# First layer's experts: three buffers for gate and up, two for down, each filled by one transfer

## The chip, the cores and the metric

The kernel runs on one core of one Trainium2 chip. The metric is the device time of one execution in microseconds (us), as the median of several runs. All matrices are in 32-bit floating point.

## The reference, cut to what matters

The model is two transformer blocks behind each other. The change lies in the mixture-of-experts part of the second block, which has two layers. Each layer routes its tokens to two of 32 experts (512 tokens in the first layer, 256 in the second), and each expert is three weight matrices of 2 MB each:

```python
def expert_block(args):
    xe, e = args
    return (jax.nn.silu(xe @ w_gate[e]) * (xe @ w_up[e])) @ w_down[e]
...
y = lax.map(expert_block, (xb, blk_e)).reshape(cap, d)
out = jax.ops.segment_sum(y.astype(jnp.float32) * w_buf[:, None], tok_buf, num_segments=t + 1)
```

`w_gate[e]` and `w_up[e]` are 1024 x 512, `w_down[e]` is 512 x 1024. With at most 64 rows for each expert the kernel makes 32 expert steps in a layer, and reads 96 matrices, 201 MB.

## The kernel before, in words

All work is written out by hand for each engine, with semaphores between them. One expert step `e` on TensorE (`pair`, L1472) is: the first half of the gate and up products (`hidden`), the transposes of the last expert's activation (`turn_act`), the second half of the gate and up products, the transposes of the next expert's rows (`turn_rows`, first layer only), and then the down products of expert `e - 1` (`down`, L1457). So the down weights of an expert are used one step later than its gate and up weights. `hidden` signals `pe_hidden`, and `down` signals `pe_y_hi`.

The weights are loaded by SyncE (SP) on one queue, in the order of its program. A buffer for one matrix is called a home. Each of the three parts (0 gate, 1 up, 2 down) has homes 0 and 1 in the six ring slots (`MOE_SLOTS`), and in the first steps of a layer also more homes in memory that is idle then: gate's home 2 is `hT`, up's home 2 is in the arena, down's home 2 is made of three rows of `more` and one of `hb`, and gate's home 3 is made of pieces, in the first layer the three rows of `bc`, `silu_fix` and a part of the arena (`gate_pieces`). A home made of pieces is filled by one transfer for each piece (`fetch_pieces`, L674): down's home 2 by four of 512 KB, gate's home 3 by three of 512 KB and two of 256 KB. All other homes are filled by one transfer of 2 MB (`fetch`, L667).

`HOMES = (4, 3, 3)` says how many homes gate, up and down have. The class `Homes` plays the first steps through (16 in the first layer, 28 in the second: `UNROLLED`) and writes the list `refills`: which matrix goes to which home, and which signal SP waits for before it (L736 to L738). After those steps each part goes by homes 0 and 1 alone, in a loop (`pair` of SP, L693): it waits for `pe_hidden` of `e` and loads gate and up of `e + 1`, then waits for `pe_y_hi` of `e - 1` and loads down of `e`. So that the loop finds its homes, the last matrices of the list must lie in the home of their number's parity (the condition `f < any_home or h == f % 2` in `freed`).

Before the first step, SP's `experts` (L661) fills all homes: homes 0 and 1 as the output projection `w_o` frees the ring, gate's home 2 and the pieces when `homes_dead` tells that the attention's memory is free (L722 to L726), and up's home 2 and the last piece of gate's home 3 after the first gathered rows have landed (L731 to L734). The rows of each expert in the first layer are gathered by GpSimd (POOL) from DRAM, and every expert's output is stored by it with an indirect DMA. The second layer gathers nothing.

Of the kernel before, what the change touches and what calls it, by code (L numbers as in the profile page):

```python
# [21 lines left out]
NB = 512  # L22
# [99 lines left out]
def build_program(nc, I, out):  # L122
    with ExitStack() as ctx:
        def sb(name, shape, dt=F32):
            return ctx.enter_context(nc.sbuf_tensor("sb_" + name, shape, dt))
# [26 lines left out]
        xs = sb("xs", [P, 4, D])  # L152
        bc = sb("bc", [P, 3, D])
# [7 lines left out]
        silu_fix = sb("silu_fix", [P, NB])  # L161
# [31 lines left out]

        MOE_SLOTS = ((2, 3, 4), (0, 1, 5))
        UNROLLED = (16, 28)
        HOMES = (4, 3, 3)

        def loop_sems(l):
            by_rows = ["places", "equals", "marked"] if l else ["rows0", "rows1", "picked_in"]
# [76 lines left out]
        for p, what in enumerate(loads):  # L276
            if 0 <= p - loads_to[0] < LAND:
                q = behind_experts[p - loads_to[0]]
            else:
                q = min(range(LAND), key=lambda q: -1 if held[q] is None else turn[held[q]])  # L280
# [15 lines left out]
        def steps_less_2(engine):  # L296

            return engine.value_load(steps_i[0:1, 0:1], min_val=N_EXP // 2 - 2, max_val=CAP // ROWS * (N_EXP // 2) - 2)

        def expert_steps(engine, v, body, l, first=True, between=None):  # L300

            if first:
                for i in range(UNROLLED[l] // 2):
                    body(i, False)
            if between:
                between()
            with engine.Fori(UNROLLED[l] // 2, v + 1) as i:
                body(i, False)
            body(v + 1, True)
# [9 lines left out]
        class Homes:  # L319

            def __init__(self, n):
                self.n = n
                self.at, self.count, self.held, self.refills = {}, {}, {}, []
                self.next = list(HOMES)
                for part in range(3):
                    for e in range(HOMES[part]):
                        self.put(part, e, 1 - e if e < 2 else e)
                for e in range(n):  # L330
                    self.freed((1, 0), "pe_hidden", e)
                    if e:
                        self.freed((2,), "pe_y_hi", e - 1)
                self.first_held = {(part, j): self.held[part, j] for part in range(3) for j in range(2)}
# [24 lines left out]

                return max(0, self.last_at(part, j) - self.first_held[part, j])  # L360

        homes = [Homes(n) for n in UNROLLED]

        def moe_home(h, part):

            return ring[MOE_SLOTS[h][part]][:] if h < 2 else (hTf, view(8192, SLOT))[part]

        def gate_pieces(l):

            if l:  # L370
                return xs[:, 2, :], xs[:, 3, :], bc[:, 1, :], bc[:, 0, :]
            return bc[:, 0, :], bc[:, 1, :], bc[:, 2, :], silu_fix[:], view(5632, NB)

        def down_rows(h):

            if h == 2:
                return more[:, 0, :], more[:, 1, :], more[:, 2, :], hb[:, 0, :]
            return [moe_home(h, 2)[:, k * D:(k + 1) * D] for k in range(4)]

        def rows_by_k(l, part, h):  # L380

            pieces = gate_pieces(l) if h == 3 else [moe_home(h, part)]
            return [v[:, at:at + NB] for v in pieces for at in range(0, v.shape[-1], NB)]

        def transfers(l, part, h):

            return len(gate_pieces(l)) if h == 3 else 4 if (part, h) == (2, 2) else 1

        def slot_of(n):

# [12 lines left out]
        def view(at, *dims):  # L403
            n = int(np.prod(dims))
            v = A[:, at:at + n]
            if len(dims) == 1:
                return v
            names = "abcde"[:len(dims)]
            return v.rearrange(f"p ({' '.join(names)}) -> p {' '.join(names)}", **dict(zip(names, dims)))
# [133 lines left out]
        def rows_of(t):  # L543

            return own_y[:, t, :, :] if t < 2 else y_rows[:, t, :, :]
# [71 lines left out]
        def _(sp):  # L617
# [43 lines left out]
            def experts(l):  # L661


                m = moe[l]
                w3 = I["w_gate_2"][l], I["w_up_2"][l], I["w_down_2"][l]

                def fetch(part, h, e):  # L667

                    src = w3[part][e:e + 1, :, :] if isinstance(e, int) else w3[part][bass.ds(e, 1), :, :]
                    src = src.rearrange("o (p k) n -> p (o k) n", p=P)  # L670
                    dst = moe_home(h, part).rearrange("p (k n) -> p k n", k=src.shape[1])
                    sp.dma_start(dst, src).then_inc(m[f"landed{3 * h + part}"], 16)  # L672

                def fetch_pieces(part, h, e, which):  # L674

                    src = w3[part][e].rearrange("(p k) n -> p (k n)", p=P)
                    at = 0
                    for q, dst in enumerate(gate_pieces(l) if h == 3 else down_rows(h)):
                        n = dst.shape[-1]
                        if q in which:  # L680
                            sp.dma_start(dst, src[:, at:at + n]).then_inc(m[f"landed{3 * h + part}"], 16)
                        at += n

                def refill(part, h, e):

                    if transfers(l, part, h) > 1:
                        fetch_pieces(part, h, e, range(transfers(l, part, h)))
                    else:
                        fetch(part, h, e)

                of = lambda n: n if isinstance(n, int) else n % N_EXP

                def pair(i, last):  # L693
                    for j in range(2):
                        e = i * 2 + j
                        if not (last and j == 1):

                            sp.wait_ge(m["pe_hidden"], e)
                            fetch(0, 1 - j, of(e + 1))
                            fetch(1, 1 - j, of(e + 1))  # L700

                        sp.wait_ge(m["pe_y_hi"], e - 1)
                        fetch(2, j, of(e))


                if l == 1:
                    sp.wait_ge(s["homes_dead"], 2)
                    fetch_pieces(0, 3, 3, range(4))
                fetch_pieces(2, 2, 2, range(3))

                n0 = first[f"w_o{l}"]
                idle = idle_at[l]
                behind = [slot_at[place["w", n0]], LAND + n0 % 2]
                waiting = [(0, 1), (1, 1), (0, 0), (1, 0), (2, 1), (2, 0)]
                for used, slots in ((turn["w", n0] + 1, idle), (turn["w", n0 + 1] + 1, behind), (uses_to[l], None)):
                    sp.wait_ge(s["w_used"], used)
                    now = [(part, h) for part, h in waiting if slots is None or MOE_SLOTS[h][part] in slots]
                    for part, h in now:
                        fetch(part, h, 1 - h)
                        waiting.remove((part, h))  # L720

                sp.wait_ge(s["homes_dead"], 1 + 2 * l)  # L722
                fetch(0, 2, 2)
                fetch_pieces(2, 2, 2, (3,))
                if l == 0:
                    fetch_pieces(0, 3, 3, range(4))  # L726
                sp.wait_ge(s["steps_ready"], l + 1)
                less_2 = steps_less_2(sp)
                steps = less_2 + 2
                if l == 0:  # L730
                    sp.wait_ge(m["rows0"], 16)  # L731
                fetch(1, 2, 2)
                if l == 0:
                    fetch_pieces(0, 3, 3, (4,))  # L734

                for part, e, h, signal, count in homes[l].refills:  # L736
                    sp.wait_ge(m[signal], count)
                    refill(part, h, e)  # L738
                expert_steps(sp, less_2, pair, l, first=False)

                def rows(t):

                    sp.dma_start(rows_of(t), DR["y"][l][2 * t * P:2 * (t + 1) * P, :].rearrange("(p j) d -> p j d", j=2)).then_inc(s[f"y_loaded{t}"], 16)

                sp.wait_ge(s["y_stored"], 1 + 2 * l)
                rows(0)
                if l == 0:
                    sp.wait_ge(m["pe_hidden"], steps * 2 - 1)
                    load(loads_to[0])
                rows(1)  # L750
                if l == 0:
                    load(loads_to[0] + 1)
                    sp.wait_ge(s["y_stored"], 2)
                    sp.wait_ge(s["own_w"], OWN_READY)
                    rows(2)
                    rows(3)
# [2607 lines left out]
```

## Time and profile before

| | us |
|---|---|
| median of 3 runs | 2381.54 (2381.46 to 2382.77) |
| the profiled execution | 2383.17 |
| its span on the core | 2381.4 |
| TensorE busy | 2163.0 (91%) |
| VectorE busy | 1108.3 (47%) |
| first layer's experts | about 1204 to 1700 |
| second layer's experts | about 1895 to 2375 |

The span is what the records of the engines cover; the execution's own time is 1.8 us more. A time in a row counts from the start of the span. "DMA share" is the mean busy share of the 16 DMA engines, and "q1" is SP's queue, "q0" that of GpSimd. The granted clock is given as a share of 2.4 GHz.

### The profile page before, as it was taken

How to read it: one execution, taken by the hardware profiler on the slowest of the kernel's cores; microseconds unless marked ns; L12 is line 12 of the kernel's file. 1: busy time of each engine (PE TensorE's matmuls, PEld its weight loads, DVE VectorE, ACT ScalarE, POOL GpSimd, SP SyncE). 2: the span in 40 equal slices, each digit the busy share in tenths (PEclk: the TensorE clock that was granted, in tenths of full speed). 3: DMA queues.
4: the chain of work that ended last, by engine and by line, in shares of the span. 5: the costliest groups of instructions: out<-in, count | busy, mean ns of one | idle time of the engine just before them, and what ended most of it. 6: DMA issues, size and time to landing. Idle time of an engine off the chain costs nothing. (4 is left out here: it accounts for less than half of the span.)

```text
span 2381.4 us, 28791 instructions
## 1 busy us (share of the span) xinstructions
PE 2163.0 (91%) x11404; PEld 1359.2 (57%) x11404; DVE 1108.3 (47%) x1760; ACT 692.2 (29%) x1102; POOL 215.2 (9%) x318
## 2 busy tenths in 40 slices
PE   8899999998899999988979887888788899999987
PEld 6778788876777888865733332333365533333332
DVE  5677654465677546477521111111488522222223
ACT  4243344344334433257111101011237211111110
POOL 2000000010000001100011111111120100000000
PEclk9989999999999999999889998999889899999999
DMA  9745576573655656611699999999861699999996
GB/s 308 257 150 188 193 237 203 173 282 126 242 204 187 216 181 215 181 51 35 254 345 393 405 411 392 406 409 407 317 151 63 239 399 425 426 425 425 426 416 274
DMA packets 186570, 657.08 MB, mean 276 GB/s; under 512 B 17511, under 2 KB 63159, under 8 KB 164304
## 3 DMA queue, kind: packets, MB, share of 16 engines
q1 hardware_dynamic: 170592, 622.66, 68.6%
q0 software_dynamic: 14032, 30.00, 4.0%
q10 hardware_dynamic: 1824, 2.73, 0.3%
q8 instruction: 86, 1.41, 0.2%
q14 instruction: 36, 0.29, 0.0%
HBM read 649.97 MB, written 23.79 MB: 283 GB/s over the span
## 5 line engine op out<-in xcount | busy, mean ns | idle before, releaser
L811 PE MATMUL bank<-sb_ring_rounded,sb_hT_rounded 128*128 128x512 f32 x2432 | 605.0, 397 | 17.0 <-DVE sb_ring_rounded L2112 6.6
L811 PEld LDWEIGHTS bank<-sb_ring_rounded,sb_hT_rounded 128*128 128x128 f32 x2432 | 458.4, 191 | 117.9 <-issue 11.8
L1443 PE MATMUL bank<-sb_ring,sb_arena 128*64 128x512 f32 x1472 | 431.3, 633 | 63.3 <-DMA sb_ring<-in_w_up 51.1
L2112 DVE TENSOR_TENSOR sb_ring_rounded<-sb_ring,sb_ring_rounded 128x2048 fp32r<-128x2048 f32 (+1 forms) x142 | 314.9, 2258 | 111.3 <-ACT sb_ring_rounded L1584 106.3
L811 PE MATMUL bank<-sb_ring_rounded,sb_arena_rounded 128*128 128x512 f32 x1408 | 356.7, 395 | 7.7 <-DVE sb_arena_rounded L2099 7.2
L1584 ACT ACTIVATE sb_ring_rounded<-sb_ring 128x2048 fp32r<-128x2048 f32 x146 | 268.0, 1887 | 123.9 <-PE bank L811 98.9
L811 PEld LDWEIGHTS bank<-sb_ring_rounded,sb_arena_rounded 128*128 128x128 f32 x1408 | 266.0, 190 | 63.5 <-DVE sb_arena_rounded L2099 7.4
L1443 PEld LDWEIGHTS bank<-sb_ring,sb_arena 128*64 128x64 f32 x1472 | 130.0, 144 | 253.3 <-issue 241.2
L1994 ACT ACTIVATE sb_hb<-bank 64x512 f32<-64x512 f32 x64 | 37.8, 591 | 659.1 <-PE bank L1443 659.1
L1467 PE MATMUL bank<-sb_ring,sb_arena 128*64 128x512 f32 x800 | 191.5, 622 | 18.6 <-issue 15.0
L2946 DVE COPY sb_arena<-bank 128x256 f32<-128x256 f32 x64 | 27.2, 424 | 279.0 <-PE bank L1454 268.9
L2969 DVE COPY sb_arena<-bank 64x512 f32<-64x512 f32 x64 | 44.4, 693 | 201.1 <-PE bank L1443 201.1
L1467 PEld LDWEIGHTS bank<-sb_ring,sb_arena 128*64 128x64 f32 x800 | 57.6, 142 | 121.6 <-issue 117.8
L1443 PE MATMUL bank<-sb_arena 128*64 128x512 f32 x232 | 104.7, 596 | 0.0
L3146 POOL DMA_INDIRECT scratch_y<-sb_arena,sb_pick x62 | 57.1, 922 | 407.4 <-DVE sb_arena L2953 178.7
L2955 DVE TENSOR_TENSOR sb_arena<-bank,sb_bc 64x512 f32<-64x512 f32 x32 | 22.2, 693 | 141.4 <-PE bank L1467 141.4
L1443 PE MATMUL bank<-sb_hT,sb_arena 128*64 128x512 f32 x176 | 79.8, 596 | 6.5 <-DMA sb_arena<-in_w_up 3.3
L2953 DVE COPY sb_arena<-bank 64x512 f32<-64x512 f32 x30 | 20.8, 693 | 122.4 <-PE bank L1467 122.4
L3216 POOL TENSOR_TENSOR sb_st<-sb_st,sb_cst 128x1 f32<-128x1 f32 x32 | 25.2, 789 | 522.8 <-DVE sb_st L2094 389.6
L1689 ACT ACTIVATE sb_hb<-bank,sb_st 128x512 f32<-128x512 f32 (+1 forms) x96 | 61.3, 652 | 19.1 <-DVE sb_st L2319 13.2
L1454 PEld LDWEIGHTS bank<-sb_cst,sb_arena 64*128 64x128 f32 x256 | 35.4, 210 | 52.7 <-issue 52.7
L1563 ACT ACTIVATE sb_hT_rounded<-bank 128x512 fp32r<-128x512 f32 x56 | 31.7, 599 | 107.4 <-PE bank L847 104.7
(376 smaller groups left out, 2379.4 us busy)
## 6 DMA issues: line engine op xcount, KB each, us to landing
sb_ring<-in_w_up SPq DMA_DIRECT2D x50, 2048.0 KB, 22.0
sb_ring<-in_w_down SPq DMA_DIRECT2D x50, 2048.0 KB, 24.1
sb_ring<-in_w_gate SPq DMA_DIRECT2D x42, 2048.0 KB, 21.9
sb_ring<-in_w_ada SPq DMA_DIRECT2D x48, 1024.0 KB, 7.3
sb_ring<-in_ffn_w_gu SPq DMA_DIRECT2D x44, 1024.0 KB, 7.8
sb_arena<-in_w_up SPq DMA_DIRECT2D x14, 2048.0 KB, 24.3
sb_hT<-in_w_gate SPq DMA_DIRECT2D x11, 2048.0 KB, 29.0
sb_more<-in_w_down SPq DMA_DIRECT2D x42, 512.0 KB, 23.9
```

Source lines behind the costliest of these rows:

```text
L811: ins = pe.matmul(bank[b][0:rows, :], rnd(x), rnd(w[:, k, :]), start=start and k == k0 and q == 0, stop=stop and k == k1 - 1 and q == len( ...
L1443: ins = pe.matmul(bank[2 * j + part][part * ROWS:(part + 1) * ROWS, :], mxT[:, j, k, :], w[part][k], start=k == 0, stop=k == KD - 1)
L1454: ins = pe.transpose(bank[2 * j][:, k * ROWS:(k + 1) * ROWS], mact[0:ROWS, j, k:EXP_H:4], ident[0:ROWS, 0:ROWS])
L1467: ins = pe.matmul(bank[S0 + n][n * ROWS:(n + 1) * ROWS, :], mactT[:, j, k, :], w[k][:, n * NB:(n + 1) * NB], start=k == 0, stop=k == 3)
L1563: act.activation(rnd(dst), bank[b][:, 0:n * P].rearrange("p (k n) -> p k n", k=n), ACT.Copy).then_inc(*c.up(s["x_hi"]))
L1584: act.activation(rnd(high_of(n)[:, k0:k1, :]), slot_of(n)[:, k0:k1, :], ACT.Copy).then_inc(*c.up(s["w_hi"]))
L1689: act.activation(j_e[:, g % 2, a, at:at + nk], bank[score_banks(g) + a][:, at:at + nk], ACT.Exp, bias=nm[:, h:h + 1], scale=query_rstd(t, ...
L1994: act.activation(msil[0:ROWS, j, :], bank[2 * j][0:ROWS, :], ACT.Silu).then_inc(m["silu"], 1)
L2112: dve.tensor_tensor(rnd(w), w, whole(high_of(n)[:, k0:k1, :]), ALU.subtract).then_inc(*c.up(s["w_lo"]))
L2946: dve.tensor_copy(mactT[:, j, :, :], bank[2 * j][:, 0:4 * ROWS].rearrange("p (k n) -> p k n", k=4)).then_inc(m["aT"], 1)
L2969: dve.tensor_copy(mup[0:ROWS, j, :], bank[2 * j + 1][ROWS:P, :]).then_inc(m["up"], 1)
L3146: pool.indirect_dma_start(out=DR["y"][l], out_offset=bass.IndirectOffsetOnAxis(ap=pick[:, 1, j:j + 1], axis=0), in_=my[0:ROWS, j, :], in_o ...
```

## The change

The first layer gets three homes for gate, three for up and two for down, in place of four, three and three. The homes made of pieces are no longer used in that layer. The second layer keeps its 4, 3 and 3 with their pieces.

```diff
-        HOMES = (4, 3, 3)
+        HOMES = ((3, 3, 2), (4, 3, 3))
...
-            def __init__(self, n):
+            def __init__(self, n, counts):
...
-                self.next = list(HOMES)
+                self.next = list(counts)
                 for part in range(3):
-                    for e in range(HOMES[part]):
+                    for e in range(counts[part]):
...
-        homes = [Homes(n) for n in UNROLLED]
+        homes = [Homes(n, counts) for n, counts in zip(UNROLLED, HOMES)]
...
-        def gate_pieces(l):
-            if l:
-                return xs[:, 2, :], xs[:, 3, :], bc[:, 1, :], bc[:, 0, :]
-            return bc[:, 0, :], bc[:, 1, :], bc[:, 2, :], silu_fix[:], view(5632, NB)
+        def gate_pieces():
+            return xs[:, 2, :], xs[:, 3, :], bc[:, 1, :], bc[:, 0, :]
...
                 if l == 1:
                     sp.wait_ge(s["homes_dead"], 2)
                     fetch_pieces(0, 3, 3, range(4))
-                fetch_pieces(2, 2, 2, range(3))
+                    fetch_pieces(2, 2, 2, range(3))
...
                 sp.wait_ge(s["homes_dead"], 1 + 2 * l)
                 fetch(0, 2, 2)
-                fetch_pieces(2, 2, 2, (3,))
-                if l == 0:
-                    fetch_pieces(0, 3, 3, range(4))
+                if l == 1:
+                    fetch_pieces(2, 2, 2, (3,))
...
                 fetch(1, 2, 2)
-                if l == 0:
-                    fetch_pieces(0, 3, 3, (4,))
```

The list of refills of the first layer becomes: up and gate of `e + 3` when the hidden products of `e` are done, down of `e + 2` when the down products of `e` are done. Its end is, with the signal and its count:

```
up, gate 15 pe_hidden 13    down 13 pe_y_hi 12
up, gate 16 pe_hidden 14    down 14 pe_y_hi 13    down 15 pe_y_hi 15 (home 1)
```

In the list before, the end is:

```
up, gate 14, pe_hidden 12 (gate 15, too)   down 14 pe_y_hi 12
up 15 pe_hidden 13    up, gate 16 pe_hidden 14    down 15 pe_y_hi 13
```

## Rows read from the trace of the kernel before

**Rows 1.** The windows view: busy time of each engine, then clock, DMA share, GB/s.
```profile
1220.00:1440.00 220.00, 193.30 (x898) 76.12 (x896) 37.41 (x60) 26.69 (x45) 31.81 (x46) 0.95 1.01 403
1480.00:1680.00 200.00, 169.03 (x748) 64.18 (x744) 30.35 (x49) 21.33 (x36) 26.86 (x49) 0.92 1.00 407
1960.00:2200.00 240.00, 237.89 (x1048) 88.09 (x1046) 65.75 (x114) 29.46 (x51) 19.83 (x35) 1.00 1.01 425
```

**Rows 2.** The waits view, TensorE, 1200 to 1700 us: total, times, longest, us.
```profile
PE bank L1443 <- DMA sb_ring<-in_w_up: 45.2, 16, 6.8
```

**Rows 3.** The timeline of TensorE, the first steps: start, duration, engine, line, operation.
```profile
1204.26 1.11 PE L1426 MATMUL bank<-sb_cst,sb_arena 64*128 64x64 f32 x8 [9.68 <-DMA sb_arena<-scratch_tokens,sb_spare]
1206.07 9.58 PE L1443 MATMUL bank<-sb_ring,sb_arena 128*64 128x512 f32 x32 [0.69 <-ACT sb_arena L1961]
...
1226.17 3.65 PE L1467 MATMUL bank<-sb_ring,sb_arena 128*64 128x512 f32 x16
...
1238.41 3.65 PE L1467 MATMUL bank<-sb_ring,sb_arena 128*64 128x512 f32 x16
```

**Rows 4.** The timeline of TensorE, the loop and the stage's end.
```profile
1492.66 3.65 PE L1443 MATMUL bank<-sb_ring,sb_arena 128*64 128x512 f32 x16 [1.80 <-DMA sb_ring<-in_w_up]
...
1508.89 6.62 PE L1443 MATMUL bank<-sb_ring,sb_arena 128*64 128x512 f32 x16 [3.76 <-DMA sb_ring<-in_w_up]
...
1692.44 3.60 PE L1467 MATMUL bank<-sb_ring,sb_arena 128*64 128x512 f32 x16
```

**Rows 5.** The timeline of SP's queue, the last fills and the first refills.
```profile
1182.58 0.33 SPq L672 DMA_DIRECT2D sb_hT<-in_w_gate  x1
1182.95 0.44 SPq L681 DMA_DIRECT2D sb_hb<-in_w_down  x1
1183.44 1.54 SPq L681 DMA_DIRECT2D sb_bc<-in_w_gate  x3
1185.02 0.46 SPq L681 DMA_DIRECT2D sb_silu_fix<-in_w_gate  x1
1204.04 0.34 SPq L672 DMA_DIRECT2D sb_arena<-in_w_up  x1
...
1215.69 0.33 SPq L672 DMA_DIRECT2D sb_ring<-in_w_up  x1
```

**Rows 6.** The DMA view, 1480 to 1680 us: packets, MB, share of 16 engines.
```profile
q1 hardware_dynamic: 5399, 78.58, 96.0%
```

**Rows 7.** The timeline of SP's queue, the list's end and the loop's first loads.
```profile
1406.62 5.18 SPq L672 DMA_DIRECT2D sb_ring<-in_w_down  x1
1431.35 0.36 SPq L672 DMA_DIRECT2D sb_ring<-in_w_gate  x1
...
1435.96 0.34 SPq L672 DMA_DIRECT2D sb_ring<-in_w_down  x1
```

**Rows 8.** The timeline of GpSimd, 1410 to 1460 us.
```profile
1438.38 1.72 POOL L3210 DMA_DIRECT2D sb_bc<-scratch_mod  x3
```

**Rows 9.** The timeline of SP's queue, the first fill of a home.
```profile
1143.77 0.33 SPq L672 DMA_DIRECT2D sb_ring<-in_w_gate  x1
```

**Rows 10.** The DMA view, 1142 to 1146 us, in slices of 0.1 us.
```profile
GB/s 0 0 0 0 0 0 0 0 0 0 0 0 0 0 0 0 0 0 0 0 0 0 0 0 0 0 0 1147 328 0 0 492 0 0 655 0 0 164 164 0
```

**Rows 11.** The timeline of GpSimd: the first gather.
```profile
1196.52 1.08 POOL L3134 DMA_INDIRECT sb_arena<-scratch_tokens,sb_spare  x1 [25.54 <-issue]
```

**Rows 12.** The tile view of the tokens in DRAM.
```profile
DMA to landing us min/median/max: 2.6/9.9/27.5
```

**Rows 13.** The windows view around the first gather.
```profile
1192.00:1200.00 8.00, 1.52 (x8) 0.90 (x8) 4.83 (x19) 0.00 (x0) 2.05 (x2) 0.63 0.99 403
1200.00:1208.00 8.00, 3.05 (x14) 1.66 (x16) 0.00 (x0) 1.88 (x2) 0.93 (x1) 0.50 0.82 152
```

**Rows 14.** The DMA view, 1220 to 1440 us.
```profile
q1 hardware_dynamic: 9234, 84.15, 95.3%
```

**Rows 15.** The timeline of SP's queue: the longest issue of pieces.
```profile
1299.11 24.50 SPq L681 DMA_DIRECT2D sb_bc<-in_w_gate  x3
```

More of the change, by code:

```diff
@@ L380, in rows_by_k @@
         def rows_by_k(l, part, h):
-            pieces = gate_pieces(l) if h == 3 else [moe_home(h, part)]
+            pieces = gate_pieces() if h == 3 else [moe_home(h, part)]
             return [v[:, at:at + NB] for v in pieces for at in range(0, v.shape[-1], NB)]
         def transfers(l, part, h):
-            return len(gate_pieces(l)) if h == 3 else 4 if (part, h) == (2, 2) else 1
+            return len(gate_pieces()) if h == 3 else 4 if (part, h) == (2, 2) else 1
         def slot_of(n):
@@ L677, in fetch_pieces @@
                     at = 0
-                    for q, dst in enumerate(gate_pieces(l) if h == 3 else down_rows(h)):
+                    for q, dst in enumerate(gate_pieces() if h == 3 else down_rows(h)):
                         n = dst.shape[-1]
```

## The prediction

> **What bounds the kernel now.** I read the page for the stages, then the windows view of the first layer's experts, then TensorE's waits there, and last the timelines of SP, TensorE and GpSimd at the two ends of the stage and where the list of refills hands over to the loop. From 1220 to 1680 us the DMA engines are full: share 1.01 and 1.00, 403 and 407 GB/s, while TensorE is busy 88% and 85% of the time at a granted clock of 0.95 and 0.92 [rows 1]. TensorE waits 45.2 us in this stage for up weights, in 16 waits [rows 2]. When nothing is late, one step takes TensorE 12.24 us (down products start at 1226.17 and at 1238.41 [rows 3]), so 32 steps would be done 392 us after 1206, near 1598; the last down products start at 1692.44 [rows 4]. So the stage is set by the bytes of SP's queue from the moment the queue is kept full, and a microsecond of idle DMA after that moment is a microsecond of the kernel. That moment is 1215.69, when the first step's gate and up products free their homes and the refills start [rows 5]. Before it the engines have slack: share 0.82 from 1200 to 1208 [rows 13].
>
> **The change, part by part.** The sum is made against the profiled execution: 2383.17 us, of which 2381.4 is the span. The median of the runs shown, 2381.54, is 1.6 us less than that execution.
>
> *Two homes less to fill ahead.* Gate 3 and down 2, 4.19 MB, were loaded before 1215.69, in time that the queue did not need. Now they are refills, behind it, and all other matrices queue as before. In the loop the queue moved 78.58 MB in 200 us [rows 6], or 0.393 MB for each us, so 2.10 MB take 5.34 us and the two 10.7 us. They lie in the path at full price, since the queue is full to the end. Bounds: 10.0 (at the 0.42 MB/us that the second layer's 425 GB/s would give [rows 1]) and 11.0 (at 84.15 MB in 220 us [rows 14]). In the first steps TensorE's pace holds: up and gate 3 are issued at 1215.69 and take 10.7 us, the third step's products need them at about 1242.
>
> *The handover.* Down has two homes, and the list must leave down 16 in home 0. So down 14 and down 15 both go to home 1, and SP waits with down 15 until the down products of expert 14 are done. Everything behind it in SP's program waits too: gate and up 17, down 16, though gate and up 17 have a free home before that. Down 14 is the last transfer in the queue then: gate and up 16 were issued a signal earlier. So the queue runs empty when down 14 has landed, and stays so for the start of the down products (some 0.3 us), their 3.65 us [rows 4], and the time from SP's issue to the first bytes, 0.9 us in the one case where the queue was empty: issued at 1143.77 [rows 9], first bytes in the slice at 1144.7 [rows 10]. With about 1 us from the last byte to the signal, an estimate, this is 6 us. Bounds: 4 (products and two short latencies at their least, and expert 14's store moving some bytes in the gap) and 9 (the clock has fallen in the wait: 16 products take 6.62 us then and not 3.65 [rows 4]). The 1.5 MB that GpSimd fetches into `bc` at this point do not fill the gap: they wait for the same down products, through expert 14's store (1438.38, right behind SP's issue at 1435.96 [rows 7, 8]). Before, nothing of this was there: down 15 was issued with expert 12's down products done, at 1406.62, and SP's pause until 1431.35 [rows 7] lay under a full queue [rows 1]. I take 6.0.
>
> *Fewer bytes in front of the first gather.* At 1182.58 SP issued gate 2 and then 2.36 MB of pieces [rows 5]. The first gather was issued at 1196.52 [rows 11], while the engines still were at 0.99 with SP's bytes [rows 13], and TensorE waited for it until 1204.26 [rows 3]. Without the pieces the queue is empty 5.6 us sooner (2.36 MB at 0.42), at about the gather's issue. The gather took 7.7 us; the shortest transfer on the same tensor took 2.6 us [rows 12]. Bounds: 0 and 5.1. I take 3, and all steps and refills start that much sooner, so it counts in full.
>
> *Whole transfers for pieces.* Gate's home 3 was refilled three times (experts 7, 11, 15) by five pieces, down's home 2 four times (5, 8, 11, 14) by four: 31 transfers become 7. While pieces were in flight the queue moved 84.15 MB in 95.3% of 220 us, 0.401 MB for each busy us; with none, 78.58 MB in 96.0% of 200 us, 0.409 [rows 14, 6]. The difference is 2% of 210 us, 4.3 us at most, and part of it comes with the denser gathers of the fast first steps. The other bound is nothing. I take 1.5 us, nearer to none: in the second layer, whose 240 us from 1960 are full of such pieces, the engines move 425 GB/s, more than here without any [rows 1]. SP's instructions for pieces that go away cost nothing: the queue is full while SP stands in them, as in the 24.50 us for three pieces [rows 15].
>
> *The rest.* The first three pieces of down 2, issued long before, left a stage with slack. VectorE, ScalarE and GpSimd do what they did. The second layer is unchanged and starts later by the sum.
>
> Sum: 10.7 + 6.0 - 3.0 - 1.5 = 12.2 us. 2383.2 + 12.2 = 2395.4 for a profiled execution, 2381.5 + 12.2 = 2393.7 for the median; I forecast 2394.
>
> **The rivals.**
>
> *Pieces are dear (faster).* Each transfer would cost the queue a time of its own that isn't under its neighbours, and 24 go. The price from a row is the 0.9 us from issue to first bytes: 24 x 0.9 = 21.6 us, so that the sum is 10.7 + 6.0 - 3.0 - 21.6 = -7.9 and the time 2373.6. It decides from 13.7 / 24 = 0.57 us for each piece. For it speaks that SP stood 24.50 us in three pieces [rows 15]. Against it speak the rates above: 31 pieces at 0.9 us would be 28 us of idle engines in 220, and the share is 1.01.
> The Trainium skill, "DMA: Bandwidth & Descriptors", section "Anatomy of one DMA", gives each DMA a fixed 2.0 us beside its bytes, and its section "Bandwidth" asks for transfers of 1 MiB and more. Taken for the queue and not for one transfer's latency, it would make 48 us of the 24, and the time about 2347; the trace has no room for this.
>
> *The gap is covered.* SP's queue does not run empty at the handover, because stores, gathers and the transfers of GpSimd fill it, or down 14 lands late enough. Then the sum is 10.7 - 3.0 - 1.5 = 6.2, the time 2388. Against it: down 15 cannot be issued before down 14 is used, whatever the speed.
>
> *TensorE becomes the bound in the first 16 steps.* With two homes, down weights land just ahead of their use, so a step waits twice. At the low clock 16 products take 6.6 us instead of 3.65 [rows 4], three such groups a step, and a step at the low clock throughout would be 12.24 + 3 x 2.97 = 21 us, above the 16 us of its bytes. If the clock fell for a third of each of the 12 steps that wait, they would have no slack left; for half of it, the excess is (12.24 + 4.5 - 16.0) = 0.7 us a step, 9 in all: 2403. Against it: a step has 3.8 us of idle in either kernel, and the clock was 0.92 with it.
>
> *Nothing changes.* The 4.19 MB would be loaded in slack again. This needs idle engines between 1216 and 1690, and there are none; only a start 12 us earlier could pay it, and the bound above is 5.1.
>
> **How the numbers follow.** Forecast 0.72, gap covered 0.10, TensorE bound 0.07, no change 0.04, pieces dear 0.07. 0.2% is 4.8 us. The ends of the forecast's terms give 10.0 + 4 - 5.1 - 4.3 = 4.6 and 11.0 + 9 = 20, so 2386 and 2401.5; the range 2386 to 2402 holds the gap's case too. Faster is the case of dear pieces, 0.07; same is the case without change, 0.04, and 0.01 from the low end of the others; slower is the rest, 0.88.
>
> **What would show it.** In the windows from 1220 to 1420 the DMA share stays 1.0, and at about 1425 to 1445 there is a dip, some 4 to 6 us in which SP's queue moves nothing, just ahead of the issue of down 15; after it no other. From the fourth or fifth step to the handover TensorE's waits stand in front of L1467, for down weights, two to four us each, and hardly any in front of L1443. The first transposes of rows start at about 1201 instead of 1204.26. The last down products of the stage start at about 1705 instead of 1692.44, and all later work is moved by as much. A share of 1.0 through the handover would refute the second term; a rate of SP's queue in the first 16 steps above 0.42 MB for each busy us would show that pieces were dear; an end of the stage before 1697 would refute the sum.

## The result, and the profile after

The changed kernel takes 2393.02 us (median of 6 runs, 2391.24 to 2401.08), the kernel before in the same rounds 2382.15. The ratio is 1.0056, with a 95% interval of 1.0041 to 1.0070: the change costs 13.3 us (9.8 to 16.7). 2394 and a cost of 12.2 us were forecast. In a second set of rounds the ratio was 1.0058 (1.0045 to 1.0071). The profiled execution of the changed kernel took 2401.08 us, with a span of 2399.2, 8 us more than the median, so I compare stretches of the two profiles and not their spans.

The stage is best measured from SP's issue of gate 2 into `hT` to the down products of expert 30, the next to last expert. (The prediction takes those, at 1692.44, for the stage's last; the last ones follow at 1698.74 before and at 1713.17 after.) Before it is 1692.44 - 1182.58 = 509.9 us [rows 4, 5]. The profile after has, in the timelines of SP and of TensorE (start, duration, engine, line, operation):

```profile
1183.51 0.33 SPq L670 DMA_DIRECT2D sb_hT<-in_w_gate  x1
1201.28 0.34 SPq L670 DMA_DIRECT2D sb_arena<-in_w_up  x1
1213.03 0.33 SPq L670 DMA_DIRECT2D sb_ring<-in_w_up  x1
```

```profile
1201.50 1.11 PE L1421 MATMUL bank<-sb_cst,sb_arena 64*128 64x64 f32 x8 [5.95 <-DMA sb_arena<-scratch_tokens,sb_spare]
...
1706.77 3.60 PE L1462 MATMUL bank<-sb_ring,sb_arena 128*64 128x512 f32 x16
...
1713.17 5.35 PE L1462 MATMUL bank<-sb_ring,sb_arena 128*64 128x512 f32 x16 [2.18 <-DVE sb_arena L2941]
```

That is 523.3 us, 13.4 more, as much as the times differ by the ratio (13.3). The spans of the two profiles differ by 17.8: 0.9 of it lie ahead of gate 2's issue and 3.5 behind the stage, where the profiles of this study also differ among kernels that do the same work there (683.5 to 692.4 us from down 30 to the end of the span). The start of the stage is 3.6 us shorter, 29.5 us from gate 2 to the first refill where it was 33.1 [rows 5]. From the first refill to the end of the issue of down 31 it is 486.7 us (1213.03 to 1699.70), where it was 469.7 (1215.69 to 1685.37). The DMA view of these two stretches (packets, MB, share of the 16 engines), the kernel before first:

```profile
q1 hardware_dynamic: 15683, 178.10, 93.9%
q0 software_dynamic: 5072, 9.15, 5.6%
```

```profile
q1 hardware_dynamic: 12507, 182.21, 91.9%
q0 software_dynamic: 5072, 9.15, 5.4%
```

SP's queue was busy for 0.939 x 469.7 = 441.0 us and is now for 447.2; GpSimd's queue is unchanged at 26.3. So of the 17.0 us more, 6.2 are bytes of SP's queue (4.1 MB more, moved at 0.407 MB for each busy us in place of 0.404), and 10.8 are share of the engines in which no queue moved anything (for a share, 1 us is 1 us of all 16 engines; the shares of all queues in these two views add up to 0.998 and 0.976, so the missing share is 0.9 us before and 11.7 after). The windows view of the changed kernel shows where (columns as in rows 1):

```profile
1220.00:1420.00 200.00, 169.04 (x768) 67.65 (x766) 31.99 (x51) 23.13 (x39) 25.28 (x37) 0.91 1.01 407
1500.00:1700.00 200.00, 168.44 (x742) 63.73 (x739) 30.49 (x50) 22.07 (x38) 26.94 (x49) 0.91 1.00 409
1432.00:1436.00 4.00, 4.00 (x22) 1.56 (x20) 0.42 (x1) 0.00 (x0) 1.59 (x2) 1.00 0.80 306
1436.00:1440.00 4.00, 2.63 (x16) 1.25 (x12) 1.38 (x2) 1.19 (x2) 0.00 (x0) 1.00 0.41 150
1440.00:1444.00 4.00, 0.00 (x0) 0.00 (x0) 0.00 (x0) 0.00 (x0) 0.18 (x1) 0.58 0.12 43
1444.00:1448.00 4.00, 3.67 (x10) 1.29 (x12) 0.00 (x0) 0.00 (x0) 0.00 (x0) 0.56 0.01 4
1448.00:1452.00 4.00, 4.00 (x22) 1.46 (x20) 0.69 (x1) 0.59 (x1) 0.73 (x1) 1.00 0.41 94
```

Full before and after, and one hole between 1432 and 1452, the handover, in which 13.0 us of share are missing (full windows read up to 1.01, so over the whole stretch it is less, 11.7). SP and TensorE in it:

```profile
1406.01 0.33 SPq L670 DMA_DIRECT2D sb_ring<-in_w_up  x1
1406.38 0.43 SPq L670 DMA_DIRECT2D sb_ring<-in_w_gate  x1
1417.78 32.14 SPq L670 DMA_DIRECT2D sb_ring<-in_w_down  x2
1450.34 0.36 SPq L670 DMA_DIRECT2D sb_ring<-in_w_gate  x1
```

```profile
1437.54 1.09 PE L1421 MATMUL bank<-sb_cst,sb_arena 64*128 64x64 f32 x8
1444.33 5.21 PE L1462 MATMUL bank<-sb_ring,sb_arena 128*64 128x512 f32 x16 [5.70 <-issue]
```

Up and gate 16 are issued at 1406, down 14 at 1417.78. Down 15 is the second of the two in the 32.14 us, at about 1449.6, when the down products of expert 14, started at 1444.33, are done. Gate 17 follows at 1450.34, though the hidden products that free its home ended about 1437.5. The hole is as forecast in its cause and in its place in SP's program; on the clock it lies at 1434 to 1451, where 1425 to 1445 was forecast. Its size is not as forecast, and the reason can be read in the DMA view of 1432 to 1452, in slices of 0.5 us:

```profile
DMA  6999795445452422123001000000100000000957
```

The share, a mean over 16 engines, falls in steps from 1434.5 to 1443 or so and not at once. I read it as engines that end one after the other (the view shows no single engine): down 14 is in place when the last has done its part. Only then do the down products begin, at the low clock level (5.21 us for what takes 3.65; the granted clock is 0.56 in 1444 to 1448, after TensorE stood for 5.70 us), and SP's next issue waits for their end. The first bytes come at about 1450.5. By these slices some 6 of the 13 us are missing before 1443 and some 7 behind it.

TensorE's waits moved as forecast. In 1220 to 1430 us, before and then after:

```profile
PE bank L1467 <- issue: 16.0, 7, 3.7
PE bank L1443 <- DMA sb_ring<-in_w_up: 4.2, 2, 2.3
PE bank L1443 <- DMA sb_arena<-in_w_up: 3.9, 2, 2.1
```

```profile
PE bank L1462 <- issue: 31.0, 10, 6.0
```

Until the handover all of them are in front of the down products now (L1462), 3.1 us each. The view names no releaser; down weights landing just then is my reading.

### The profile page after: what moved, and what is told of

It reads as the page before. It is cut to its first block and busy times, and to the rows that moved or that the text cites. A ratio compares the mean times of both kernels' runs of the same rounds, so it can differ in the third digit from the quotient of the medians.

```text
span 2399.2 us, 28758 instructions
## 1 busy us (share of the span) xinstructions
PE 2170.0 (90%) x11404; PEld 1364.6 (57%) x11404; DVE 1108.7 (46%) x1760; ACT 692.3 (29%) x1102; POOL 216.3 (9%) x318
## 5 line engine op out<-in xcount | busy, mean ns | idle before, releaser
L1438 PE MATMUL bank<-sb_ring,sb_arena 128*64 128x512 f32 x1520 | 415.3, 629 | 57.0 <-DMA sb_ring<-in_w_up 49.6
L1438 PEld LDWEIGHTS bank<-sb_ring,sb_arena 128*64 128x64 f32 x1520 | 126.6, 144 | 257.1 <-issue 248.2
L1462 PE MATMUL bank<-sb_ring,sb_arena 128*64 128x512 f32 x880 | 217.7, 640 | 44.6 <-issue 40.3
L1462 PEld LDWEIGHTS bank<-sb_ring,sb_arena 128*64 128x64 f32 x880 | 66.2, 146 | 161.9 <-issue 158.2
L1438 PE MATMUL bank<-sb_hT,sb_arena 128*64 128x512 f32 x192 | 87.0, 595 | 2.6 <-DMA sb_ring<-in_w_up 1.3
L3211 POOL TENSOR_TENSOR sb_st<-sb_st,sb_cst 128x1 f32<-128x1 f32 x32 | 25.2, 791 | 523.2 <-DVE sb_st L2089 389.5
L1684 ACT ACTIVATE sb_hb<-bank,sb_st 128x512 f32<-128x512 f32 (+1 forms) x96 | 61.2, 652 | 18.3 <-DVE sb_st L2314 13.3
## 6 DMA issues: line engine op xcount, KB each, us to landing
sb_hT<-in_w_gate SPq DMA_DIRECT2D x12, 2048.0 KB, 29.5
```

The costliest lines, as they stand in the source:

```text
L1438: ins = pe.matmul(bank[2 * j + part][part * ROWS:(part + 1) * ROWS, :], mxT[:, j, k, :], w[part][k], start=k == 0, stop=k == KD - 1)
L1462: ins = pe.matmul(bank[S0 + n][n * ROWS:(n + 1) * ROWS, :], mactT[:, j, k, :], w[k][:, n * NB:(n + 1) * NB], start=k == 0, stop=k == 3)
L1684: act.activation(j_e[:, g % 2, a, at:at + nk], bank[score_banks(g) + a][:, at:at + nk], ACT.Exp, bias=nm[:, h:h + 1], scale=query_rstd(t, ...
```

## The experiments

Each ratio is against the kernel before in the same rounds; 0.0010 is 2.4 us. "Stage" is the stretch defined above.

| kernel | ratio (95%) | median us | stage us |
|---|---|---|---|
| before | 1 | 2380.13 to 2383.34 in four sets | 509.9 |
| changed | 1.0056 (1.0041 to 1.0070) | 2393.02 | 523.3 |
| changed, again | 1.0058 (1.0045 to 1.0071) | 2395.88 | 523.6 |
| parity | 1.0033 (1.0020 to 1.0046) | 2388.27 | 514.8 |
| parity_wait | 1.0068 (1.0056 to 1.0080) | 2397.59 | 523.2 |
| free_first | 1.0017 (1.0007 to 1.0027) | 2387.06 | 515.1 |
| quarters | 1.0081 (1.0068 to 1.0094) | 2403.33 | 534.8 |
| three_each | 0.9996 (0.9985 to 1.0007) | 2381.04 | 511.9 |
| three_late | 1.0005 (0.9995 to 1.0014) | 2381.56 | 508.8 |
| late_pieces | 0.9991 (0.9982 to 1.0000) | 2379.20 | 508.7 |
| late_pieces, again | 0.9999 (0.9989 to 1.0009) | 2379.60 | 507.4 |

**The changed kernel again.** No edit.

> The changed kernel once more, beside its variants, to measure how large the idle stretch at the handover is in another execution. My theory: its profile again shows the DMA engines running out one after the other at about 1435 to 1451 us, 10 to 13 us of idle share there, and a time 11 to 14 us above the kernel before. If the long stretch of the first profile was a chance of that execution, the idle share is about 6 us.

The hole is there again. The windows view from 1428 to 1456, the kernel before first, then this run:

```profile
1428.00:1456.00 28.00, 20.17 (x100) 7.49 (x96) 4.57 (x7) 3.56 (x6) 6.30 (x11) 0.95 1.00 391
```

```profile
1428.00:1456.00 28.00, 22.71 (x98) 8.84 (x96) 3.61 (x6) 2.37 (x4) 4.90 (x8) 0.88 0.47 177
```

From first refill to the issue of down 31 the idle share is 12.1 us, beside 11.7 in the first profile and 0.9 in the kernel before. So the first profile's hole was no chance of one execution; the 6 us were my error. Both profiled executions lie above the median of their runs, by 8 and 5 us. The price of the wait in a typical run is read from the medians below.

**The wait taken away by the homes' order.** Down 0 goes to home 0 and down 1 to home 1, so even experts lie in home 0 as the loop wants it, and down 15 waits for expert 13.

```diff
-                        self.put(part, e, 1 - e if e < 2 else e)
+                        self.put(part, e, e if counts[part] == 2 or e > 1 else 1 - e)
...
-                        fetch(part, h, 1 - h)
+                        fetch(part, h, h if (l, part) == (0, 2) else 1 - h)
```

> The changed kernel with down's two homes filled the other way round (down 0 in home 0, down 1 in home 1), so that down 15 goes to home 1 and down 16 to home 0 as they come free, and down 15 waits for the down products of expert 13 and not of 14. Theory (the wait at the handover empties the queue, and its cost in the first profile was 12 us of idle engines): the stretch is gone, the DMA share stays 1.0 from 1216 to 1680, and the time is 10 to 12 us below the changed kernel, 1 to 4 us above the kernel before. By the size I forecast it is 6 us below the changed kernel. Rival (two homes less make the queue run dry by themselves, whatever the order): the time stays with the changed kernel, 13 us above the kernel before.

```profile
1428.00:1456.00 28.00, 25.97 (x120) 10.28 (x116) 5.02 (x9) 3.60 (x7) 6.08 (x10) 0.94 0.98 377
```

The hole is gone, with two homes for down as before, so the rival that two homes run dry by themselves has fallen. The kernel is 5.9 us below the changed one by the ratios (0.0025 of 2382) and 7.6 below that of its own rounds by the medians, 8.5 in the stage: less than the 10 to 12 that I expected from the idle share. What stays, 7.9 us (4.8 to 11.0), is more than the 1 to 4 expected; in the stage it is 4.9. The prediction's own sum without the handover, 10.7 - 1.5 - 3.0 = 6.2 us, lies between the two.

**The wait alone, put back.** The kernel with the other parity, and one line.

```diff
                 for part, e, h, signal, count in homes[l].refills:
+                    if (l, part, e) == (0, 2, 15):
+                        count = 15
```

> The kernel with down's homes the other way round, in which SP waits with down 15 until the down products of expert 14 are done though its home is free before: the wait at the handover alone, put back. Theory: the idle stretch is back in the same place with 10 to 13 us of idle share, and the time is 10 to 12 us above the kernel without the wait, equal to the changed kernel. Rival (the homes' order matters, not the wait): within 2 us of the kernel without the wait.

```profile
1428.00:1456.00 28.00, 22.86 (x103) 8.53 (x99) 3.68 (x7) 2.44 (x5) 5.90 (x9) 0.88 0.52 194
```

The hole is back and the medians are 9.3 us apart (2388.27 and 2397.59), the stages 8.4. The wait is the cause, alone and without the order of the homes. It costs 8 to 9 us, while the idle share differs by 11 (12.2 and 1.0 us): part of the idle stretch is got back. The profiles show where. For the same 182.1 MB SP's queue is busy for about 446.7 us with the wait and 448.6 without, and from the issue of down 31 to the down products of expert 30 it is 7.1 us with the wait and 8.1 without. Why the queue is a little quicker with the hole isn't shown.

**What stands behind the waiting transfer.** The changed kernel with homes and wait as they are; SP issues gate and up 17 first.

```diff
+                    if (l, part, e) == (0, 2, 15):
+                        continue
...
-                expert_steps(sp, less_2, pair, l, first=False)
+                    sp.wait_ge(m["pe_hidden"], 16)
+                    fetch(0, 1, 17)
+                    fetch(1, 1, 17)
+                    sp.wait_ge(m["pe_y_hi"], 15)
+                    fetch(2, 1, 15)
+                    fetch(2, 0, 16)
...
```

> The changed kernel with its homes and the wait of down 15 as they are, but SP issues gate and up 17, whose home is free when the hidden products of 15 are done, ahead of down 15 and not behind it. Theory (the cost is what stands behind the waiting transfer, in a queue that then runs empty, and not down 15 itself): the idle share falls from 12 us to 2 to 4, and the kernel is 5 to 8 us below the changed one, close to the kernel with the other parity. Rival (down 15 late is what costs, since its down products and all behind them wait for it): no gain, or slower, since it now comes 10 us later.

```profile
1428.00:1432.00 4.00, 4.00 (x20) 1.50 (x18) 0.69 (x1) 0.59 (x1) 0.00 (x0) 0.88 0.88 377
1432.00:1436.00 4.00, 4.00 (x22) 1.58 (x20) 0.42 (x1) 0.00 (x0) 1.88 (x2) 1.00 0.67 259
1436.00:1440.00 4.00, 3.47 (x20) 1.53 (x16) 1.37 (x2) 1.09 (x2) 0.00 (x0) 1.00 0.53 131
1440.00:1444.00 4.00, 2.00 (x7) 0.74 (x9) 0.00 (x0) 0.10 (x1) 0.18 (x1) 0.83 0.86 346
```

The idle share is 2.9 us and the kernel is some 9 us below the changed one (ratios 1.0017 and 1.0056), 8.2 in the stage. The gain is a little more than the 5 to 8 expected. Down 15 lands no sooner: TensorE waits 3.87 us for it, where the changed kernel waits 0.62, and its products start 277.7 us from gate 2's issue and not 275.3. This costs nothing that can be seen, since the stage is as long as that of the kernel with the other parity (515.1 and 514.8). What cost was the free home that SP could not fill, because it stood in another wait.

**The price of a transfer.** Every matrix of the first layer's experts comes in four transfers, in the changed kernel.

```diff
-                    sp.dma_start(dst, src).then_inc(m[f"landed{3 * h + part}"], 16)
...
+                    for q in range(4):
+                        sp.dma_start(dst[:, q * n:(q + 1) * n, :], src[:, q * n:(q + 1) * n, :]).then_inc(m[f"landed{3 * h + part}"], 16)
```

> The changed kernel in which each matrix of the first layer's experts comes by four transfers of 512 KB (4 KB for each partition, as the pieces of the kernel before) and not by one of 2 MB: 96 matrices, 288 transfers more. Theory (a piece costs little): between the two kernels SP's queue went from 0.400 to 0.406 MB for each busy us in the first steps, 1.4%, with 7 of about 40 matrices in pieces, so with all in pieces the rate falls by at most 8% and the kernel is 0 to 35 us slower than the changed kernel; I expect about 10. Rival (a transfer costs the queue 0.9 us of its own): some 260 us slower, and the DMA share falls far below 1.

SP's queue from 1220 to 1420, the kernel before, the changed one, and this one:

```profile
q1 hardware_dynamic: 8583, 76.40, 95.2%
```

```profile
q1 hardware_dynamic: 5322, 77.47, 95.2%
```

```profile
q1 hardware_dynamic: 20775, 75.64, 97.1%
```

288 transfers more, 264 of them behind the first refill, cost 6 us by the ratios (1.0081 and 1.0056, from two sets of rounds) and 11.5 in the stage, so 0.02 to 0.04 us each; about 10 were expected. In the same 200 us the queue moves 2.4% less than in the changed kernel, 75.64 MB and not 77.47. Pieces are not dear: the 24 transfers that the change saves are worth 1 us at most by this price. The kernel before moved 76.40 MB, 1.4% less than the changed one, which is 2.8 us in these 200; so most of that difference is not the pieces' price. The smaller transfers also change what the other queue gets. The times from issue to landing of the 36 transfers on the tokens in DRAM, 32 of them gathers, in the changed kernel and in this one:

```profile
DMA to landing us min/median/max: 2.6/9.9/28.2
```

```profile
DMA to landing us min/median/max: 2.6/6.4/12.7
```

**One home less than before.** Three homes each: the changed kernel, to which down's home 2 with its four pieces is given back (and their issues, not shown).

```diff
-        HOMES = ((3, 3, 2), (4, 3, 3))
+        HOMES = ((3, 3, 3), (4, 3, 3))
```

> Three homes for each part in the first layer: gate's home of five pieces is gone, down's home of four pieces stays. The list has no wait of the kind of down 15's then. Theory (each home taken away costs one matrix of queue time, 5.3 us, less the pieces that no longer stand before the first gather): no idle stretch at the handover, and about 1 to 4 us above the kernel before. Rival (gate's fourth home costs nothing, all is down's third home): within 1 us of the kernel before or below it.

No difference from the kernel before can be measured (0.9996, 0.9985 to 1.0007), where a loss of 1 to 4 us was expected; in the stage 2.0 us are lost. So gate's fourth home was worth about nothing in total, its bytes against the sooner start: the first transposes come 17.9 us behind gate 2's issue (1181.92 and 1199.83), as in the changed kernel. The rest of what the changed kernel loses stands on down's third home: its absence costs the wait, and without the wait the difference between this kernel and the one with the other parity, 0.0037 or 9 us (5 to 13) by the ratios of two sets, 2.9 in the stage. The two measures do not agree, and which is nearer isn't shown: the stage is from one profile each, and the rest of the span differs between these two profiles by more than the stage does (683.5 and 690.5 us behind it).

**The pieces behind the first gather.** The kernel before, and 2.36 MB issued later.

```diff
-                fetch_pieces(2, 2, 2, (3,))
-                if l == 0:
-                    fetch_pieces(0, 3, 3, range(4))
+                if l == 1:
+                    fetch_pieces(2, 2, 2, (3,))
...
                 fetch(1, 2, 2)
                 if l == 0:
-                    fetch_pieces(0, 3, 3, (4,))
+                    fetch_pieces(2, 2, 2, (3,))
+                    fetch_pieces(0, 3, 3, range(5))
```

> The kernel before (4, 3 and 3 homes) with one thing moved: the fourth piece of down's home 2 and the first four pieces of gate's home 3, 2.36 MB, are issued behind up's home 2, when the first gathered rows have landed, and not before them. Theory (the pieces stand in the way of the first gather): the first transposes of rows start 3 to 4 us sooner after the routing and the kernel is 3 to 4 us faster than before, 2378 to 2379. Rival (the gather's time is its own): no change in either. A third way: the queue is busy at the first refill and those 2.36 MB delay it, and the gain is given back.

```profile
1181.99 0.33 SPq L672 DMA_DIRECT2D sb_hT<-in_w_gate  x1
```

```profile
1200.02 1.11 PE L1426 MATMUL bank<-sb_cst,sb_arena 64*128 64x64 f32 x8 [6.02 <-DMA sb_arena<-scratch_tokens,sb_spare]
```

> The kernel before with its pieces issued behind the first gathered rows, once more, to tell its gain from none: 1 to 3 us below the kernel before, with the first transposes at 18.0 us from the issue of gate's home 2 and not at 21.7.

The first transposes start 18.0 us (17.8 in the second profile) from gate 2 in place of 21.7: the pieces did stand before the gather, for 3.7 us. But of the 3.7 us only 1.2 and 2.5 are left at the end of the stage in the two profiles, and the ratios are 0.9991 (to 1.0000) and 0.9999 (0.9989 to 1.0009). The 3 to 4 us that I expected of the first run, and most of the 1 to 3 of the second, did not come. A gain of more than 2.6 us in the second set is excluded; whether there is one at all stays open.

The same with three homes each moves the 0.5 MB of down's last piece alone:

> Three homes for each part in the first layer, and the fourth piece of down's home 2 (0.5 MB) issued when the first gathered rows have landed. With three homes each the first transposes came 17.9 us after the issue of gate's home 2 already, as in the changed kernel, so the piece was not in the gather's way: within 1 us of the kernel with three homes each, 0 to 3 us below the kernel before. If the engines' uneven ends make the gather wait for that piece, 1 us more is gained.

1.0005 (0.9995 to 1.0014) beside 0.9996, with the first transposes at 18.0 us: no difference. No kernel of this study beats the kernel before by more than can be measured.

## Why the prediction was right, and what in it was off

*What bounds the kernel.* Right. The kernels' stages follow the bytes of SP's queue and the time in which it has none. That a microsecond of idle DMA is a microsecond of the kernel is a little too much: 11.2 us of idle share cost 8.4 in the stage (parity and parity_wait).

*Two homes less to fill ahead, and whole transfers for pieces: 10.7 - 1.5 = 9.2 us.* SP's queue was busy 6.2 us more. The bytes came out as forecast, 4.1 MB more, worth 10.2 us at the old 0.404. The rate was better than assumed, 0.407, worth 4.0 us over 182 MB; my value for the pieces was 1.5 and my bound 4.3. That all of it is the pieces is not shown: their price by the kernel in quarters accounts for about 1 us, and kernels with whole transfers alone show 0.406 (other parity) to 0.408 (with the wait) over the same stretch. The rest stays open. Without the hole (parity) SP's queue is busy 7.6 us more than before, nearer to the 9.2.

*The handover: 6.0 us.* Right in place, cause and sign, wrong in size: this is the term that was mis-sized. The queue had 10.8 us more of idle share, and the wait by itself costs 9.3 us between medians, 8.4 in the stage, at the end of my bound of 9. Of the 6.0, the 0.9 us from SP's issue to the first bytes came out (1449.6 to 1450.5); the 1 us from the last byte to the signal was an estimate with no row under it, and no run shows it apart. I took the queue's end for a point in time, as if all 16 engines put down their last bytes together. They seem to end over some 9 us, the products wait for the last, and only my 6 us of products and latencies start then, some 7 with the low clock. The bound had the low clock in it but not the slow end. [rows 1, 2] could not show it, since a full queue hides that the engines stand at different places; but the kernel before drains its queue too, at the stage's end, where down 31 waits for its home, and there the view from 1675 to 1695 has the same stairs, from 1679.5 until the bytes of down 31 begin at about 1686:

```profile
DMA  7999999995433433112223926989899799000000
```

*Fewer bytes before the first gather: 3 us.* Right: 3.6 in the stage. What it is worth in the kernel's time is less sure, by the run in which it is the only edit.

The sum then reads 6.2 + 10.8 - 3.6 = 13.4 us for 12.2 forecast, and 13.3 between the ratios. These three are stretches and shares of one measured stage, so that they add up to it proves nothing. That the total came out within 1.2 us is in part luck: two errors, a hole 4.8 us longer and a queue 3.0 us shorter in its bytes, took most of each other away. *Pieces are dear* would have shown 0.9 us for each transfer; it is at most 0.04, with the rate hardly touched. The fixed 2.0 us of the Trainium skill ("DMA: Bandwidth & Descriptors", "Anatomy of one DMA"), which the section gives for transfers that GpSimd issues and of which it calls most completion latency, cannot be a price of SP's queue for each transfer: by these runs that is at most 0.04 us in a full queue. *The gap is covered* and *nothing changes* fell with the hole and the ratio. *TensorE becomes the bound* did not come: clock and share from 1220 to 1420 are 0.91 and 1.01, as the waits moved to the down products. The clock did fall, from 0.96 in the same window before, but the queue stayed full. (The price of this rival is a little off: with the low clock for a third of each step the step takes 12.24 + 3.0 = 15.2 us, which still leaves 0.8 below the 16.0 of its bytes.)

## What to carry to other kernels

When a stage is bound by one queue, count the bytes behind the moment from which the queue is kept full, and then look for each place where its issuer waits with a transfer while a home for a later one is free: there the queue runs dry, and what stands behind the wait costs more than the waiting transfer itself. With a ring of homes that ends in a loop, let each matrix go to the home that the loop will look for from the first one on, so that the handover has no wait of its own. An emptied queue cost more here than latency and the work that it waited for: its share fell over some 9 us, not at once.

## What the runs showed of the hardware that was not expected

- The share of the 16 DMA engines falls over many microseconds when a long-filled queue runs out: from 1434.5 to 1443 at the handover of the changed kernel, and from 1679.5 at the end of the stage before, where it has not reached zero when new bytes come at 1686. While the queue is full the share is 1.0 and nothing of it shows.
- Loads of 2 MB in four transfers of 4 KB for each partition cost 2.4% of what the queue moves (75.64 and 77.47 MB in 200 us), and at most 0.04 us for each transfer more. In return GpSimd's transfers on the tokens land sooner behind the full queue: after 6.4 us in the median and 12.7 at most, where it was 9.9 and 28.2. No kernel here shows that this shortens the stage.
- The first gather lands 3.7 us sooner when 2.36 MB less are queued before it on another queue, and no sooner when 0.5 MB of these, left there alone, are taken away too (18.0 us from gate 2's issue to the first transposes, and 17.9 with them).
